# Long convolution of a 12-layer stack: another order of spectra, products, norms and inverse transforms on three engines, and other PSUM banks

## The reference, cut to what matters

```
v, x1, x2 = split(depthwise_conv3(h @ w_in, short_w, short_b), 3)
h_full    = filters from a small MLP, each channel divided by sum(|h_full|)
long_conv(u, n) = irfft(rfft(u, 512) * rfft(h_full[n], 512))[:256] + u * f_skip[n]
z = x1 * long_conv(v, 0)
z = x2 * long_conv(z, 1)
y = z @ w_out
```

## Time and profile before

| | us |
|---|---|
| median of 3 runs | 2022.86 |
| lowest and highest | 2021.9 and 2024.41 |
| the profiled execution | 2023.78 |
| its span, first to last instruction | 2022.0 |
| TensorE busy in the span | 1967.4 |
| VectorE busy in the span | 1275.0 |
| ScalarE busy in the span | 907.3 |
| mean granted TensorE clock | 0.996 |

### The profile page before, as it was taken

How to read it: one execution, slowest core, us unless ns; L and a number is a source line. 1 busy time by engine, 2 the same in 40 slices (tenths; PEclk the granted TensorE clock), 3 DMA queues, 4 the chain that set the end, 5 groups by cost and what they waited for, 6 DMA issues and landing times.

```text
span 2022.0 us, 30699 instructions
## 1 busy us (share of the span) xinstructions
PE 1967.4 (97%) x12630; PEld 1604.2 (79%) x12630; DVE 1275.0 (63%) x1623; ACT 907.3 (45%) x1284; POOL 160.5 (8%) x198
## 2 busy tenths in 40 slices
PE   7999999999899999999999999999999999999999
PEld 6689788878678878888878678877767888898887
DVE  7874855567765565755767665577886555475554
ACT  4452344434444434444545454434434444444442
POOL 2242100000010010000003011002100000000000
PEclk9999999999999999999999999999999999999999
DMA  8411365646156654565465347653332556454554
GB/s 298 123 52 58 104 215 195 219 152 214 53 175 206 224 176 169 175 188 187 166 192 189 109 134 225 200 185 128 105 125 93 181 195 218 159 194 156 187 168 155
DMA packets 93044, 335.97 MB, mean 166 GB/s; under 512 B 11230, under 2 KB 11364, under 8 KB 92623
## 3 DMA queue, kind: packets, MB, share of 16 engines
q1 hardware_dynamic: 85824, 311.62, 45.9%
q0 software_dynamic: 7120, 22.95, 4.2%
HBM read 332.43 MB, written 1.05 MB: 165 GB/s over the span
## 4 chain that ended last, share of the span: by engine, by line
PE 87%; DVE 8%; ACT 2%; POOL 1%; issue 1%; DMA 0%; SPq 0%; DVEq 0%; ACTq 0%; POOLq 0%
PE acc L420 43%; PE acc L506 20%; PE acc L477 8%; DVE w_lo L1660 2%; PE acc L978 2%; PE aux L899 1%; PE aux L526 1%; PE aux L683 1%; POOL rstd L2507 1%; PE aux L966 1%; DVE w_spare_lo L1660 1%; PE aux L934 1%; PE acc L670 1%; ACT w_hi L1238 1%; POOL rstd L2510 1%
## 5 line engine op out<-in xcount | busy, mean ns | idle before, releaser
L1660 DVE TENSOR_TENSOR w_lo<-w_raw,w_hi 128x1024 fp32r<-128x1024 f32 x552 | 670.3, 1225 | 527.7 <-ACT w_hi L1238 524.1
L1238 ACT ACTIVATE w_hi<-w_raw 128x1024 fp32r<-128x1024 f32 x552 | 580.0, 1059 | 714.7 <-PE acc L420 438.3
L420 PE MATMUL acc<-w_hi,operand_hi 128*128 128x512 f32 x1232 | 488.8, 397 | 14.5 <-DVE operand_lo L1843 12.3
L420 PE MATMUL acc<-w_hi,operand_lo 128*128 128x512 f32 x1232 | 481.8, 391 | 0.0
L420 PE MATMUL acc<-w_lo,operand_hi 128*128 128x512 f32 x1232 | 481.2, 391 | 0.0
L420 PEld LDWEIGHTS acc<-w_hi,operand_hi 128*128 128x128 f32 x1232 | 231.9, 188 | 63.3 <-DVE operand_lo L1843 12.1
L420 PEld LDWEIGHTS acc<-w_hi,operand_lo 128*128 128x128 f32 x1232 | 231.7, 188 | 49.1
L420 PEld LDWEIGHTS acc<-w_lo,operand_hi 128*128 128x128 f32 x1232 | 232.2, 188 | 46.8 <-issue 0.5
L506 PE MATMUL acc<-w_hi,hidden_hi 128*128 128x512 f32 x528 | 207.9, 394 | 0.0
L506 PE MATMUL acc<-w_hi,hidden_lo 128*128 128x512 f32 x528 | 205.9, 390 | 0.0
L506 PE MATMUL acc<-w_lo,hidden_hi 128*128 128x512 f32 x528 | 205.6, 389 | 0.0
(11 more groups left out here) (485 smaller groups left out, 2432.5 us busy)
## 6 DMA issues: line engine op xcount, KB each, us to landing
w_raw<-in_weights SPq DMA_DIRECT2D x552, 512.0 KB, 3.5
w_spare_raw<-in_weights SPq DMA_DIRECT2D x36, 512.0 KB, 5.2
ln_gain<-in_gains POOLq DMA_DIRECT2D x7, 512.0 KB, 4.5
bias_at<-in_rpb POOLq DMA_DIRECT2D x12, 256.0 KB, 4.7
ln_gain<-in_ln_g POOLq DMA_DIRECT2D x4, 512.0 KB, 4.2
ln_bias<-in_ln_b POOLq DMA_DIRECT2D x4, 512.0 KB, 5.6
vec_rw<-in_vec POOLq DMA_DIRECT2D x3, 512.0 KB, 5.4
l_rw<-in_lora SPq DMA_DIRECT2D x1, 1152.0 KB, 10.5
```

What stands on the lines that cost most here:

```text
L420: mm = pe.matmul(acc[:, 2 * pair + t, :], (ah, al)[x][:, kt, t * P:(t + 1) * P], weight(w, q + i)[:, kk * 512:(kk + 1) * 512], start=(kt = ...
L1238: act.activation(weight(0, q), raw_of(q), ACT.Copy).then_inc(hi_of(q)[0], 1)
L1660: dve.tensor_tensor(weight(1, q), raw_of(q), weight(0, q).bitcast(F32), ALU.subtract).then_inc(lo_of(q)[0], 1)
```

## The change

On TensorE the pieces stand in other steps. `spectrum(0,1,0)` changes place with the first taps of filter 1; `norm(0)` now waits for `filt_done` ahead of it, and the last taps of filter 1 follow it; `dft(0,1)` moves from (2,3) to (2,1), `spectrum(0,0,1)` from (2,1) to (2,3), `norm(1)` from (4,2) to (2,2); `idft(0,0)` from (3,3) to (3,2); `idft(0,1)` from (5,0) to (4,1), `turn_cv(3)` with it; the three spectra of filter 1 that shared (4,3) and (5,3) spread over (4,2), (4,3) and (5,1); `dft(1,0)` from (5,1) to (4,2), `dft(1,1)` from (5,2) to (5,0), `dft(1,2)` from (5,3) to (5,2), and `dft(1,3)` from behind the blocks to (5,3). New is that (4,0) waits for `idft_done` and (4,3) for `freq_done` and `idft_done`. `turn_cv(5)` follows the last inverse transform and no longer stands inside it. VectorE and ScalarE follow: `even_odd_weights(1)` comes behind the first split, `larger(1)` in (1,3), `scale_taps(1)` in (2,2), `gated(0,0)` in (3,3), `gated(0,1)` in (4,2), `products(1,0)` in (4,3), `products(1,3)` ahead of `convolve(5)`. No operation is added, removed or resized.

More of the change, by code:

```diff
@@ L255, in dft_banks @@
     def dft_banks(n, r):
-        return ((HI, LO, HI, LO), (HI, HI, LO, HI))[n][r]
+        return ((HI, LO, HI, LO), (LO, LO, LO, HI))[n][r]
     def idft_banks(n, c):
-        return ((LO, LO), (NEAR, LO))[n][c]
+        return ((HI, FAR), (NEAR, LO))[n][c]
     def cv_banks(j):
-        return (HI, HI, HI, HI, LO, FAR)[j]
+        return (HI, HI, NEAR, LO, NEAR, FAR)[j]
     def spectrum_banks(f, part, c):
-        return (LO, LO, LO, LO, HI, LO, HI, NEAR)[spectrum_order(f, part, c)]
-    def spectrum_order(f, part, c):
-        return 4 * f + 2 * (1 - part) + c
+        return (LO, HI)[f]
     def norm_bank(f):
-        return (aux[:, 0, :], acc[:, 2, :])[f]
+        return (aux[:, 2, :], acc[:, 2, :])[f]
     def tables(n):
@@ L1103, in dft, with idft @@
                 mm.then_inc(m["dft_ready"], 1)
-            def idft(n, c, between=None):
+            def idft(n, c):
                 sides = idft_banks(n, c)
@@ L1109, in idft @@
                     pe.matmul(sides[:, x, :], tables(4 * x), FR[:, 2 * x, cols_of(c)], start=True, stop=False)
-                if between:
-                    between()
                 for x in range(2):
@@ L1186, in inside_block @@
+                    turn_cv(4)
                 elif (j, i) == (5, 2):
-                    free(m["idft_done"])
-                    turn_cv(4)
                     free(m["dft_done"])
-                    dft(1, 1)
+                    dft(1, 2)
                 elif (j, i) == (5, 3):
-                    spectrum(1, 0, 1)
-                    free(m["cv_copied"])
-                    dft(1, 2)
-            def last_turn():
-                turn_cv(5)
-                free(m["dft_done"])
+                    free(m["freq_done"])
@@ L1209, in hyena @@
                 block_channels(q + 4 * j, j % 2, operand_waits=(j == 0), after={i: lambda i=i: inside_block(j, i) for i in range(4)})
-            free(m["dft_done"])
-            dft(1, 3)
-            free(m["freq_done"])
+            free(m["cv_copied"])
             idft(1, 0)
-            free(m["dft_done"])
-            idft(1, 1, between=last_turn)
+            free(m["dft_done"], m["dft_done"])
+            idft(1, 1)
+            turn_cv(5)
             for t in range(TT):
@@ L1604, in absolute @@
                     act.activation((SIZES, OTHERS[f])[a // 2][:, a % 2, :], EO[f][:, a, :], ACT.Abs).then_inc(m["taps_abs"], 1)
-            def second_sizes():
-                act.wait_ge(m["filt_done"], due(m["filt_done"], 8))
-                absolute(1)
             def copy_first_half(n, c):
@@ L1613, in copy_first_half, with turned_and_sizes, turned_and_side, spectrum_and_turned @@
                 act.activation(FIRST_HALF[n][c], idft_banks(n, c)[:, 0, :], ACT.Copy).then_inc(m["half_copied"], 1)
[L1615 to L1625, removed]
+            def turned_and_sizes():
+                copy_cv(0)
+                act.wait_ge(m["filt_done"], due(m["filt_done"], 8))
+                absolute(1)
+            def turned_and_side(c):
+                copy_cv(2 + c)
+                copy_first_half(0, c)
+            def spectrum_and_turned():
+                copy_even(1, 0, 1)
+                copy_cv(4)
             act.wait_ge(m["hyena_in"], due(m["hyena_in"], 16 * HYENA_LOADS))
             act.wait_ge(m["filt_done"], due(m["filt_done"], 0) + 4)
-            inside = {(0, 0): lambda: absolute(0), (2, 1): spectrum_and_sizes, (4, 0): sides_and_spectrum, (4, 3): two_spectra, (5, 0): lambda: copy_first_half(0, 1)}
-            inside.update({(j, 2): lambda j=j: copy_cv(j - 1) for j in range(1, 6)})
-            spectra = {(0, 1): (0, 1, 0), (0, 3): (0, 1, 1), (1, 3): (0, 0, 0), (5, 3): (1, 0, 1)}
+            inside = {(0, 0): lambda: absolute(0), (1, 2): turned_and_sizes, (2, 2): lambda: copy_cv(1), (3, 2): lambda: turned_and_side(0),
+                      (4, 1): lambda: turned_and_side(1), (5, 1): spectrum_and_turned}
+            spectra = {(0, 1): (0, 1, 0), (0, 3): (0, 1, 1), (1, 3): (0, 0, 0), (2, 3): (0, 0, 1), (4, 0): (1, 1, 0), (4, 2): (1, 0, 0), (4, 3): (1, 1, 1)}
             inside.update({at: lambda which=which: copy_even(*which) for at, which in spectra.items()})
@@ L1639, in hyena @@
             copy_first_half(1, 0)
+            copy_first_half(1, 1)
             copy_cv(5)
-            copy_first_half(1, 1)
             both_operands()
@@ L2433, in inside_block @@
                     scale_taps(0)
+                    window(1, 1, 1, 0)
                 elif (j, i) == (1, 2):
-                    window(1, 1, 1, 0)
+                    fold(0)
                 elif (j, i) == (1, 3):
-                    fold(0)
+                    larger(1)
                     butterfly(0, 0, 0)
@@ L2441, in inside_block @@
                 elif (j, i) == (2, 1):
-                    butterfly(0, 0, 1)
[L2443 to L2447, removed]
+                    products(0, 1)
+                elif (j, i) == (2, 2):
+                    scale_taps(1)
+                    fold(1)
+                elif (j, i) == (2, 3):
+                    butterfly(0, 0, 1)
                 elif (j, i) == (3, 0):
@@ L2477, in hyena @@
                 convolve(j)
-            products(1, 3)
             gated(1, 0)
```

2 lines of the change are left out of this document (removed).

## The result

The changed kernel takes 2032.33 us (median of 6 runs, 2030.02 to 2033.53) beside 2023.62 us for the kernel before (6 runs). The ratio is 1.0042, 95% interval 1.0032 to 1.0052: 8.7 us slower. I had forecast slower, by 4.4 us, and the time lies above my range of 2021 to 2031.

What follows compares the result with a forecast made beforehand. The prediction took TensorE, busy 97% of the span, as the bound, with VectorE a near second. Its terms, −5.4 + 9.8 + 4.3 − 6.9 + 2.6 = +4.4 us, gave 2027.3 us from 2022.9; range 2021 to 2031.

Steps and rivals of the forecast that it cites:

- Waits that go: TensorE's waits of 1.89, 2.89 and 0.59 us in the long convolution disappear, together −5.4 us.
- Waits that come: New TensorE waits on VectorE in the long convolution, whose pieces stand behind splits, together +9.8 us.
- (0,2): In this step TensorE waits for the window that now stands behind a butterfly, +0.9 us.
- (2,2): In this step TensorE waits for products(0,0), +1.0 us; a GpSimd side effect was bounded at 0 to +1 us.
- (4,0): In this step TensorE waits for the first idft_done, from VectorE's gated(0,0), +3.3 us.
- (4,3): In this step TensorE waits for the sixth freq_done, from butterfly(1,0,0), +3.7 us.
- (1,1): In this step TensorE waits for the window of step (1,0), asked for one quarter earlier, +0.9 us.
- Moved out of the tail: spectrum(1,0,1) and one dft move from behind quarter (5,3) to ahead of its end, +4.3 us there.
- the tail: From the end of quarter (5,3) to the turn of the result, 14.1 us in place of 21.0, −6.9 us.
- Clock: TensorE's old low-clock stretch goes, −1.7 us, and new ones follow the two longest new waits, +4.3: +2.6 us.
- The faster rival: VectorE meets the waits in (4,0) and (4,3) in time, unheld by splits; sum −6.9, about 2016 us; chance 0.10.
- At nothing: ScalarE, PSUM banks, SP's order and GpSimd's second-filter operations, taken to cost no time.

Runs made afterwards that it cites:

- e2: Changed kernel, with VectorE doing gated(0,0) one step earlier, ahead of the split instead of behind it; ratio 1.0023 to the kernel before.
- e3: Changed kernel, with VectorE doing butterfly(1,0,0) one step earlier, behind gated(0,1) and ahead of the split; ratio 1.0033 to the kernel before.
- e1: Changed kernel, with GpSimd's add for the first filter held until VectorE's split of step (0,3) is done; ratio 1.0034 to the kernel before.
- e7: Kernel before, with GpSimd's add and product of the second filter held until products(0,3) is done; ratio 0.9987 to the kernel before.
- e4: Changed kernel, with TensorE's three long waits, in (1,1), (4,0) and (4,3), filled with matmuls without use; ratio 1.0013 to the kernel before.
- e8: Kernel before, with only spectrum(0,1,0) and filter 1's first taps exchanged and even_odd_weights(1) behind the first split; ratio 0.9994 to the kernel before.
- e10: Changed kernel, with two matmuls without use filling only TensorE's wait in (1,1); ratio 1.0024 to the kernel before.
- e5: Changed kernel, with GpSimd's first add later and gated(0,0) and butterfly(1,0,0) each a step earlier, together; 2021.5 us, ratio 0.9983.

## Why the prediction went wrong, by its own steps

*Waits that go*: right, −5.4 us, all three are gone.

*Waits that come*: (0,2) 0.96 for 0.9, (2,2) 1.21 for 1.0, (4,0) 3.47 for 3.3, (4,3) 3.79 for 3.7, each with the releaser named; (5,1) none, as said. That they come from standing behind a split is shown for (4,0) by e2 and for (4,3) by e3. **(1,1) failed: 2.59 for 0.9.** The chain of VectorE was right in its links and wrong in one duration, the split of (0,3), taken at 1.14 and measured at 2.96. I had seen a VectorE instruction stretched beside GpSimd, and bounded it at 0 to +1 us in (2,2), with `convolve` as the nearest row. I hadn't walked GpSimd's queue: the exchange in (0,0) makes `larger(0)` end 2 us earlier and at the same time lets VectorE stand idle 0.6 us for the next split, in which GpSimd gets ahead. The term was 1.7 us short. e1 takes the collision away, and the wait falls to 1.39; the 0.5 above my 0.9 is the 8-column addition, 0.71 for 0.17. I had also asked why the splits beside GpSimd's pair weren't stretched, and missed the order of starts: in the kernel before the split (1400.55) started 0.17 us ahead of the add, and it was the add that took 3.32.

*Moved out of the tail* and *the tail*: right. From the last `dft` at 1519.42, at whose first matmul quarter (5,3) has ended, to the turn at 1533.67 there are 14.2 us against 14.1. Of the 6.9 us some 1.4 are the low clock in the tail of before, which not every execution has: in e7 the same tail, at full clock in its last inverse transform, is 1.4 us shorter.

*Clock*: **the larger miss.** I had +2.6. From start to start, beside the same pieces at full clock in e4, the slow stretches cost 3.1 us in (1,1) (norm 1.7, taps 0.9, the quarter behind 0.5), 2.6 in (4,0) and 1.7 in (4,3), 7.4 together. That of before cost 1.4 beside e8, the wait of 0.77 left out, so the term is +6.0. For (4,0) and (4,3) I had 4.3 and got 4.3, but that is luck: I had taken 1.7 for the first and 2.6 for the second, and it was the other way round. The 3.1 at (1,1) were missing because its wait was sized too short to matter. By the medians e10 gives 3.6 us for this one alone, e4 5.9 for all.

The sum with the measured terms is −5.4 + 12.0 + 4.3 − 6.9 + 6.0 = +10.0 at the turn; the trace has 1533.67 − 1523.87 = 9.8. Behind it 1.2 come back, as the output projection of the kernel before began at low clock (the turn takes 2.65 there and 1.97 after) and this one did not: 8.6, the difference of the profiled executions. My two misses, 1.7 and 3.4, are together more than the 4.2 us between forecast and result. By the trace both come from the one split: its wait, and 3.1 us of slow matmuls behind that wait. By the medians this isn't shown, since e1 gave back only 1.6 us; there the wait of 1.39 remains, behind which the clock can still fall.

The faster rival was refuted where I had said it would be decided. Its remedy was right all the same: e2 and e3 free the two pieces from their splits, and with e1 the kernel falls below both.

*At nothing*: GpSimd's pair of the second filter cost nothing, as said. At 1428.4 and 1430.9 it lies beside the butterfly and `convolve(1)`, and only one 8-column addition grew, by 0.13 us. That the PSUM banks alone cost nothing was not tested by a run; the sum above leaves 0.2 us for all that it doesn't name.

## What to carry to other kernels

When a hand-ordered queue changes, walk GpSimd's instructions forward as carefully as the others and ask which engine starts first; a stretch of 1.7 us on a piece that nobody waits for costs nothing (e8), and the same stretch ahead of a new wait cost over 4 us by the traces (e1 against the changed kernel: 1.2 of wait, 3.1 of clock). Price a wait of TensorE together with the slow stretch that may follow it: here some 6 us (e4) behind three waits of 9.9 in sum. A piece that others wait for belongs ahead of the split in the queue if its inputs are there, not in the same step behind it.

## What the runs showed of the hardware that I had not expected

A VectorE and a GpSimd instruction that both read two SBUF tensors did not run at the same time: the one that started second ended about its own length, less 0.1 us, behind the end of the other (the split 1.08 us behind, GpSimd's add 2.27). VectorE: the split 2.96 for 1.22, the subtraction 1.65 for 0.69, an 8-column addition 0.71 for 0.17. GpSimd: 3.26 and 3.32 for 2.38. `convolve`'s long instructions and the butterflies, which read one tensor in PSUM and one in SBUF, kept their length in the same microseconds. The Trainium skill, "VectorE: DVE Perf Modes", section "Two Vector instructions with no wait between them", says that the two engines share the second SBUF read interface; these rows agree, and show that here it was not shared bit by bit: in each pair the second waited until the first had ended.

Low clock came irregularly. It followed a wait of 1.38 us in e5 (the norm took 2.62) and not one of 1.39 in e1 (2.00); it followed 2.89 in the kernel before and neither 1.95 in e7 nor 2.90 in e8. The wait of 2.6 in (1,1) was followed by it in all three traces that have it unfilled (the changed kernel, e2, e3). Executions of one kernel spread over 5 us (e1: 2027.4 to 2032.7). One profiled execution doesn't size it; filling the wait does.
